# A hybrid decoder step on one core: cached values requested two half samples earlier, and retention's head norm run head by head with the first output unit's second part beside it

## The reference, cut to what matters

```python
idx = indexer_topk(iq, iw, ik_all, pos, k_sel)          # samples: keys and values in pages of 128 rows
kg = jnp.where(in_past, ck[page, off], k[bi, nidx])
vg = jnp.where(in_past, cv[page, off], v[bi, nidx])
att = sparse_attend(q, kg, vg, idx, pos, rel_bias)
...
mu = jnp.mean(o, axis=-1, keepdims=True)                # o: retention's output, per head of 128
var = jnp.mean(jnp.square(o - mu), axis=-1, keepdims=True)
on = ((o - mu) * lax.rsqrt(var + EPS)).reshape(b, l, H_R * DV_R)
ret = jax.nn.silu(rg) * on.astype(rg.dtype)
return jnp.concatenate([att.reshape(b, l, H_A * DH_A), ret], axis=-1) @ w_out
```

## Time and profile before

| | before |
|---|---|
| runs, us | 3350.01, 3346.58, 3349.80; median 3349.8 |
| profiled execution, us | 3346.32 |
| its span, us | 3344.6 |
| mean granted TensorE clock | 0.979 |
| PE busy | 3206.0 us, 96% |
| DVE, ACT, POOL busy | 45%, 34%, 36% |
| DMA over the span | 263.89 MB, mean 79 GB/s |

### The profile page before, as it was taken

The page is one execution under the profiler, slowest core; times in us unless marked ns, Lnnn a source line. Parts: engine busy times, 40 slices in busy tenths (PEclk is TensorE's granted clock), DMA queues, the critical chain, the costliest instruction groups (busy, mean ns, idle before and its releaser), DMA issues. The chain is left out here.

```text
span 3344.6 us, 56689 instructions
## 1 busy us (share of the span) xinstructions
PE 3206.0 (96%) x20604; PEld 3038.7 (91%) x20604; DVE 1497.6 (45%) x2630; ACT 1147.9 (34%) x2142; POOL 1205.1 (36%) x890
## 2 busy tenths in 40 slices
PE   7899989989999999999999999999899999999998
PEld 6589975679999999999999889898899999999997
DVE  3699974542312121223476676776722212121222
ACT  3511225633313121223445455545432313122222
POOL 2217834314222222223356654546533222222122
PEclk9999989989999999999999999999999999999998
DMA  4237646123111111113232222331431111111111
GB/s 138 56 32 167 201 154 216 63 97 52 44 44 50 44 44 50 44 45 101 72 97 81 69 85 83 96 102 38 166 135 44 46 49 44 51 44 47 47 44 70
DMA packets 344007, 263.89 MB, mean 79 GB/s; under 512 B 52134, under 2 KB 308150, under 8 KB 341910
## 3 DMA queue, kind: packets, MB, share of 16 engines
q1 hardware_dynamic: 328502, 233.23, 23.3%
q0 software_dynamic: 8192, 19.13, 1.7%
q10 hardware_dynamic: 7200, 10.04, 1.5%
HBM read 219.43 MB, written 44.76 MB: 79 GB/s over the span
## 5 line engine op out<-in xcount | busy, mean ns | idle before, releaser
L234 POOL TENSOR_TENSOR w_low_sb<-w_loaded_sb,w_high_sb 128x1024 fp32r<-128x1024 f32 (+1 forms) x278 | 569.3, 2055 | 1523.2 <-ACT w_high_sb L226 1505.3
L252 PE MATMUL psum<-act_high_sb,w_high_sb 128*128 128x344 f32 (+1 forms) x2400 | 770.0, 321 | 6.5 <-PEq L2819 3.2
L252 PE MATMUL psum<-act_low_sb,w_high_sb 128*128 128x344 f32 (+1 forms) x2400 | 768.3, 320 | 0.0
L252 PE MATMUL psum<-act_high_sb,w_low_sb 128*128 128x344 f32 (+1 forms) x2400 | 768.1, 320 | 0.0
L252 PE MATMUL psum<-second_high_sb,w_high_sb 128*128 128x344 f32 x1728 | 553.3, 320 | 0.5 <-PEq L2410 0.5
L252 PE MATMUL psum<-second_low_sb,w_high_sb 128*128 128x344 f32 x1728 | 551.9, 319 | 0.0
L252 PE MATMUL psum<-second_high_sb,w_low_sb 128*128 128x344 f32 x1728 | 551.9, 319 | 0.0
L252 PEld LDWEIGHTS psum<-act_high_sb,w_high_sb 128*128 128x128 f32 (+1 forms) x2400 | 451.1, 188 | 7.8 <-issue 5.7
L252 PEld LDWEIGHTS psum<-act_high_sb,w_low_sb 128*128 128x128 f32 (+1 forms) x2400 | 451.5, 188 | 0.4
L252 PEld LDWEIGHTS psum<-act_low_sb,w_high_sb 128*128 128x128 f32 (+1 forms) x2400 | 451.2, 188 | 0.4
L226 ACT CAST w_high_sb<-w_loaded_sb 128x1024 fp32r<-128x1024 f32 (+1 forms) x230 | 239.4, 1042 | 524.8 <-PE psum L252 497.8
(11 more groups left out here) (436 smaller groups left out, 4722.7 us busy)
## 6 DMA issues: line engine op xcount, KB each, us to landing
w_loaded_sb<-in_w_up SPq DMA_DIRECT2D x64, 512.0 KB, 4.1
w_loaded_sb<-in_w_down SPq DMA_DIRECT2D x64, 512.0 KB, 3.6
w_loaded_sb<-in_w_in_odd SPq DMA_DIRECT2D x48, 512.0 KB, 3.9
key_pages_sb<-in_cache_k SPq DMA_DIRECT2D x64, 256.0 KB, 3.1
ecay_sum_spread_sb<-decay_sum_scratch SPq DMA_DIRECT2D x8, 2048.0 KB, 9.9
w_loaded_sb<-in_w_in_even SPq DMA_DIRECT2D x28, 512.0 KB, 4.0
value_pages_sb<-in_cache_v SPq DMA_DIRECT2D x56, 256.0 KB, 6.1
gated_scratch<-gated_sb POOLq DMA_DIRECT2D x8, 1032.0 KB, 4.4
```

Source lines behind the costliest of these rows:

```text
L234: ins = self.nc.gpsimd.tensor_tensor(self.wl[:, par, k, 0:width], self.wf[:, par, k, 0:width], self.wh[:, par, k, 0:width].bitcast(F32), A ...
L252: ins = nc.tensor.matmul(out, w[:, par, k, 0:width], a[:, k, cols], start=n == 0, stop=n == 3 * KT - 1)
```

## The change

In row turning, SP asks for half samples 2 and 3 at once, and for half sample 4 after five of the eight k rows have been stored. In attention, SP begins with half sample 5; the store of the v rows comes after the last request. `AHEAD` becomes 5.

In retention's norm, ACT casts head h - 1 right after the exponential of head h, DVE makes every low part itself, that of head h - 1 after the product of head h, and POOL has no work. PE goes on in the same block with parts 4 to 7 of output unit 0, each when its head's high and low part exist; `ProjectAdd` then begins with parts 4 to 7 of unit 1.

```diff
--- before.py
+++ after.py
@@ -1284,7 +1284,7 @@
     HALVES = NS * PAGES // HALF
     KRING = 3
     VRING = 6
-    AHEAD = 3
+    AHEAD = 5
     AHEAD_ACT = 2
     FIRST = 7
     BANKS = (1, 7, 3)
@@ -1693,7 +1693,10 @@
             sp.dma_start(B.bias[:], bass.AP(tensor=B.bias_rows.tensor, offset=P - 1,
                                             ap=[[HA * 384 - 1, P], [384, HA], [1, 2 * P]])).then_inc(s_biast, 16)
             smp.load_values(sp, 2)
+            smp.load_values(sp, 3)
             for b in range(NBLK):
+                if b == 5:
+                    smp.load_values(sp, 4)
                 await_kept(sp, 3 + b)
                 sp.dma_start(B.o["k_prompt"][0, 0, b * P:(b + 1) * P].rearrange("p h d -> p (h d)"),
                              kn[:, b, :]).then_inc(B.s_k, 16)
@@ -1852,11 +1855,11 @@
     with nc.Block() as block:
         @block.sync
         def _(sp):
+            for m in range(smp.AHEAD, smp.HALVES):
+                smp.load_values(sp, m)
             sp.dma_start(B.o["v_prompt"][0, 0].rearrange("(n p) h d -> p n (h d)", p=P), B.vn[:]).then_inc(B.s_v, 16)
             sp.dma_start(B.o["k_sample"][0].rearrange("b o h d -> (b o) (h d)"), B.qkv_s[:, 1, :]).then_inc(B.s_v, 16)
             sp.dma_start(B.o["v_sample"][0].rearrange("b o h d -> (b o) (h d)"), B.qkv_s[:, 2, :]).then_inc(B.s_v, 16)
-            for m in range(smp.AHEAD, smp.HALVES):
-                smp.load_values(sp, m)
             rotary.load(sp, smp)
             sp.wait_ge(B.s_v, 48)
             sp.wait_ge(rotary.s_values, 16)
@@ -2259,7 +2262,6 @@
 
     oc = r[:, 4:8, :]
     sq = sw
-    LOW_DVE = (1, 3)
     s_sum, s_oc, s_sq, s_sum2, s_ln, s_rs, s_og, s_on, s_hi, s_lo = (B.sem(x) for x in (
         "head_summed", "centred", "centred_square", "square_summed", "deviation_log", "inverse_deviation", "gated",
         "gated_normed", "ret_high", "ret_low"))
@@ -2302,6 +2304,10 @@
                 if (first + e) % 2 == 1:
                     pe.wait_ge(s_ln, HR)
                 B.multiply_part(pe, B.unit + e, (first + e) % 2, B.hh, B.hl, range(HR))
+            for h in range(HR):
+                pe.wait_ge(s_hi, h + 1)
+                pe.wait_ge(s_lo, h + 1)
+                B.multiply_part(pe, B.unit, first, B.hh, B.hl, range(HR + h, HR + h + 1))
 
         @block.vector
         def _(dve):
@@ -2320,8 +2326,9 @@
                 dve.wait_ge(s_og, h + 1)
                 dve.wait_ge(s_rs, h + 1)
                 nc.vector.tensor_tensor(o[:, h, :], r[:, 8 + h, :], sq[:, h, :], ALU.mult).then_inc(s_on, 1)
-            for h in LOW_DVE:
-                low(h)
+                if h >= 1:
+                    low(h - 1)
+            low(HR - 1)
 
         @block.scalar
         def _(act):
@@ -2335,19 +2342,16 @@
                     square(h + 1)
                 act.wait_ge(s_sum2, h + 1)
                 nc.scalar.activation(wide(sq[:, h, :]), B.psum[:, 3:6, 0:TT], ACT.Ln, bias=B.eps[:, 0:1], scale=1.0 / DVR).then_inc(s_ln, 1)
+            def high(h):
+                act.wait_ge(s_on, h + 1)
+                nc.scalar.copy(B.hh[:, 4 + h, :], o[:, h, :]).then_inc(s_hi, 1)
+
             for h in range(HR):
                 act.wait_ge(s_ln, h + 1)
                 nc.scalar.activation(sq[:, h, :], sq[:, h, :], ACT.Exp, scale=-0.5).then_inc(s_rs, 1)
-            for h in range(HR):
-                act.wait_ge(s_on, h + 1)
-                nc.scalar.copy(B.hh[:, 4 + h, :], o[:, h, :]).then_inc(s_hi, 1)
-
-        @block.gpsimd
-        def _(pool):
-            for h in range(HR):
-                if h not in LOW_DVE:
-                    pool.wait_ge(s_hi, h + 1)
-                    nc.gpsimd.tensor_tensor(B.hl[:, 4 + h, :], o[:, h, :], B.hh[:, 4 + h, :].bitcast(F32), ALU.subtract).then_inc(s_lo, 1)
+                if h >= 1:
+                    high(h - 1)
+            high(HR - 1)
     B.top = mark
 
 
@@ -2383,7 +2387,7 @@
 
     def pe(self, pe):
         B, U0 = self.B, self.U0
-        for e in range(AHEAD):
+        for e in range(1, AHEAD):
             B.multiply_part(pe, U0 + e, (U0 + e) % 2, B.hh, B.hl, range(HR, KT))
         with pe.Fori(1, 4) as j:
             for e in range(2):
```

## The result

The changed kernel takes 3331.2 us (median of five, 3328.4 to 3331.9), the kernel before 3350.0 in the same comparison: a ratio of 0.9939 with a 95% interval of 0.9924 to 0.9953, so 16 to 25 us less. The forecast was 12.7 less and 3337. Faster was right; the size was not, and scaled to the median of 3349.8 the ratio gives 3329.4, under the range's low end of 3331.

What follows compares the result with a forecast made beforehand. Taken as bound by PE, busy 96%: attention -7.8, row turning 0 and norm -4.9 sum to -12.7 us, from the profiled 3346.3 to 3333.6, or 3337 against the median of 3349.8; range 3331 to 3343.

Steps and rivals of the forecast that it cites:

- The two waits: Attention's start: PE's waits for half samples 3 and 4, 2.27 + 2.55 us, both go, 4.8 us gained.
- The slow clock: Attention, 508.4 to 515.7: the slow clock follows the two waits and goes with them, 3.0 us gained, ends 0 and 3.2.
- rival 1: Early attention: the clock does not come back, a slow stretch appears elsewhere; 3.0 us less gain, 3340; chance 0.17.
- Row turning: Eight more pages there: ACT's first group -1.4 us, second +1.2, sum 0; ends -3.6 and +4.4.
- Rivals 2 and 4: Row turning: ACT's loads slowed by stores and traffic, +4.4, 3341.5, chance 0.12; or 4.0 us each, 3363, chance 0.03.
- Retention's norm: Norm to output units: DVE's low parts at 1.22 us, unit 0's adds earlier, -4.9 us, ends -3.5 and -5.5.
- Rival 3: Norm: low parts stay at 3.3 us on DVE, +1.5 in place of -4.9, 3343.5; chance 0.04.
- Rival 5: Attention: half sample 5 or 6 is waited for as long as half sample 3 was, 3342; chance 0.08.
- The chances: Whole kernel: faster (under 3343.1) 0.85, same 0.12, slower 0.03; the forecast itself got 0.52.

Runs made afterwards that it cites:

- k_stores_later: Changed kernel with the eight k stores moved into attention behind half sample 5, half sample 4 asked for straight behind 3: 3330.0 us, ratio 0.9930 to before.
- v_store_last: Kernel before with only the v rows' store moved behind attention's last request, half samples 3 and 4 still asked for there: attention 141.5 us.
- pool_low: Changed kernel with the low parts of heads 0 and 2 back on GpSimd: units 26.5 us against 26.0, one profile.
- sp_asks: k_stores_later with SP requesting half samples 0 to 3 in row turning, ACT none; 4, 5 and k stores open attention: 3328.4 us (0.9932), then 3328.8 (0.9936).

## Why the prediction was wrong, and where it was right

- **The two waits (4.8 us): right** in size. On average over the five profiles of the old code it was 4.4. The reason was half of it. I took the waits to go because the pages are requested earlier, and cost the v store's move at nothing. The runs show that the store's move alone, or the requests' alone, is enough, since either takes the register loads out from behind the store.
- **The slow clock (3.0, "between ends of 0 and 3.2"): the step that failed.** The clock came back, and rival 1 fell. But 3.2 was no upper end: it was the length of the stretch in one profile. Two of the kernel's three further profiles lost 3 us more there. The stage's gain is 9.2 on average instead of 7.8, and without the 4.4 of the waits it leaves 4.8 for the slow clock where the forecast had 3.0. This is the term that was mis-sized: a loss that differs between executions was taken from one profile, and that profile had one of the shorter stretches. The sentence of the Trainium skill (TensorE: Matmul & The Clock Gate, What's actually happening), that slow matmuls vary from run to run, stood next to it; I used it only for the case that the gain stays away, and it speaks for a larger loss before as well. The traces agree with it: attention took 149.6 to 152.5 us in five profiles with the same two waits.
- **Row turning (0, ends -3.6 and +4.4): right in its ends, too small by about 1.2 us** on average (part of which may be the clock's, see above) and by 3.8 in the first pair. The first group went from 5.00 to 3.60, as worked out. The second was to get longer behind five stores and got shorter, 3.91: the stores, issued from 473.86, took 6.5 to 9.0 us to land behind the pages queued ahead of them, so most of ACT's loads were done before the stores slowed anything; in another profile of the same code, started a little differently, the second group met them, with loads of 0.83, 1.05 and 0.77 us, and row turning took 23.9. That stores and not traffic slow the loads was right, shown by `k_stores_later` and `v_store_last`. Rivals 2 and 4 fell: no load on ACT was over 1.52 us in any kernel.
- **Retention's norm (-4.9): right**, with its steps: low parts 1.23 us, gap 1.66, PE never waits between heads, POOL's chain decides; 5.0 us on average. Rival 3 fell. The Trainium skill's rule (SBUF — State Buffer, SBUF: two separate sides) is borne out by `pool_low`: whichever of the two started second took longer, 2.25 and 2.54 us instead of 1.22 on DVE, 3.40 instead of 2.44 on POOL.
- **Rival 5: fell.** No value page was waited for.
- **The chances: one sum is off.** By the forecast's own parts faster comes to 0.82 and same to 0.15, not to 0.85 and 0.12.
- **What stays open.** The timed difference is 18.7 to 20.3 us between medians in four comparisons, with intervals that begin at 14 to 16. The stages account for 15.4 and the profiled spans for 16.0. Some 3 to 4 us are not located, but the timed executions show which kernel they belong to and what they go with. The profiled executions of the changed kernel took 3331.3 us on average, as its others did; those of the kernel before took 3347.3, 3 us less than the median of all its timed executions, and had a mean clock of 0.979 or 0.980. Over some 70 timed executions of the kernel before the clock was 0.978 on average, and the time went with it: 3354 us at 0.976, 3346 at 0.980. So a usual execution of the kernel before loses more to the slow clock than the profiles that the forecast and the stages were read from. In which stretch it does so, no run here shows.

Of the versions tried, `sp_asks` is in front of the changed kernel by 4.0 and 2.1 us between medians in two comparisons. Its row turning (18.4 us in both profiles against 22.3) says the same; the intervals of the ratios overlap, so it is the likelier one and not a proven one. Of `sp_asks` and `k_stores_later` neither is shown to be in front.

## What to carry to other kernels

Before crediting a load's new place, ask what its queue was held up by: here register loads behind the issue and the transfer of a store of 2 MB, and moving the store was worth as much as moving eight requests. An idle gap of 2 us on TensorE may cost as much again in slow clock behind it, and how much is not to be read from one profile: take several before using such a stretch as a bound. A free engine is not always a help: here GpSimd's low parts held up those of DVE, and DVE alone was 0.5 us faster in the one profile that compares them.

## What the runs showed that I had not expected

- A TENSOR_LOAD of one number from SBUF takes 0.27 us on SP and 0.29 on ACT, also while pages come in at 385 GB/s (`k_stores_later`, 467 to 476 us), but up to 1.9 us where a store from SBUF has been issued and has not yet landed; some loads there stay at 0.3. In the same place the slow loads repeat to 1%: 1125, 870 and 1899 ns in the profile of before, 1127, 870 and 1911 in the next.
- The stretch from the norm's first sum to the units takes 20.5 to 20.9 or 22.2 to 22.7 us, nothing between, in all 20 profiles and in either kernel, at a clock of about 0.91 or 0.80. Such steps of 2 us are in every comparison of single profiles.
